# Value stage: 768 gathered and 1280 dense columns, and the coefficients' low halves made by GpSimd

## The reference, cut to what matters

```python
def peer_ffn(x, wq, subkeys, u, v):          # x: 256 tokens x 2048
    ...                                      # 8 heads x 16 experts = 128 slots per token, out of 16384
    act = gelu(einsum('td,tkd->tk', xc, u[ec]))
    return einsum('tk,tkd->td', gc * act, v[ec])
```

## Time and profile before

| | us |
|---|---|
| median of 3 runs | 1769.39 (1768.2 to 1777.46) |
| profiled execution, its own time | 1779.1 |
| its span (first to last instruction) | 1777.3 |
| value stage in it, first issue to last product | 1188.4 to 1671 |
| busy over the span: PE, DVE, ACT, GpSimd | 1265.5, 1466.0, 808.6, 873.6 |

### The profile page before, as it was taken

One profiled execution on the slowest core, in us unless ns is written; L12 is line 12 of the kernel. 1 busy time (PEld: TensorE's weight loads), 2 busy tenths in 40 slices (PEclk: granted clock), 3 DMA queues, 4 the chain that ended last, 5 costly groups with the idle time before them and its releaser, 6 DMA issues.

```text
span 1777.3 us, 22600 instructions
## 1 busy us (share of the span) xinstructions
PE 1265.5 (71%) x7003; PEld 1129.7 (64%) x7003; DVE 1466.0 (82%) x1984; ACT 808.6 (45%) x1403; POOL 873.6 (49%) x872
## 2 busy tenths in 40 slices
PE   9999999999992460000122222399999999999997
PEld 9899998989982430000111122289999999999887
DVE  6636666754578998999999999889999999999856
ACT  6324446644210121111777777684444444444654
POOL 1100000000154546666766677488888888888303
PEclk9999999999996685555555555599999999999999
DMA  9954444367899999999999999819999999999953
GB/s 303 332 196 147 143 143 143 121 235 263 317 372 422 417 404 423 413 409 422 421 421 416 414 414 422 360 50 383 378 381 376 383 376 378 379 373 382 349 192 117
DMA packets 120101, 577.12 MB, mean 325 GB/s; under 512 B 14596, under 2 KB 29269, under 8 KB 78688
## 3 DMA queue, kind: packets, MB, share of 16 engines
q0 software_dynamic: 58544, 367.16, 51.1%
q1 hardware_dynamic: 61488, 209.10, 32.9%
HBM read 571.99 MB, written 7.36 MB: 326 GB/s over the span
## 4 chain that ended last, share of the span: by engine, by line
PE 59%; DVE 12%; DMA 11%; issue 10%; POOL 5%; ACT 1%; SPq 1%; DVEq 0%; POOLq 0%; ACTq 0%
PE banks L2339 17%; PE banks L2346 9%; PE banks L1929 7%; DVE rows L1695 6%; DMA rows<-peer_u_dram,expert 6%; PE banks L1985 6%; PE banks L2008 5%; PE banks L2230 4%; DMA early_rows<-peer_u_dram,expert 3%; PE banks L1987 3%; PE banks L2312 2%; POOL rows L797 2%; PE banks L1949 1%; DVE early_rows L1695 1%; POOL pick L739 1%
## 5 line engine op out<-in xcount | busy, mean ns | idle before, releaser
L1695 DVE SCALAR_TENSOR_TENSOR rows<-rows,banks 128x2048 f32<-128x2048 f32 x206 | 466.2, 2281 | 39.2 <-DMA rows<-peer_u_dram,expert 38.5
L849 POOL DMA_INDIRECT vrow<-peer_v_gathered_dram,vidx x224 | 342.6, 1529 | 73.1 <-issue 44.9
L797 POOL DMA_INDIRECT rows<-peer_u_dram,expert x206 | 197.7, 960 | 340.1 <-DVE expert L1732 154.2
L2312 PE MATMUL banks<-hots 128*128 128x128 f32 x512 | 103.0, 370 | 233.8 <-ACT hots L1239 229.5
L2312 PEld LDWEIGHTS banks<-hots 128*128 128x128 f32 x512 | 90.2, 266 | 246.8 <-issue 177.8
L1797 DVE SCALAR_TENSOR_TENSOR hres<-vrow,slot_coef,hres 128x704 f32<-128x704 f32 x224 | 211.9, 946 | 4.5 <-DMA vrow<-peer_v_gathered_dram,vidx 4.2
L1811 DVE TENSOR_TENSOR vlo<-vraw,vhi 128x1344 fp32r<-128x1344 f32 x128 | 198.8, 1553 | 2.2 <-ACT vhi L1287 1.7
L913 ACT CAST whi<-raw 128x2048 fp32r<-128x2048 f32 x77 | 146.8, 1906 | 116.0 <-PE banks L1929 67.3
L2339 PE MATMUL banks<-vhi,chi 128*128 128x448 f32 x762 | 179.2, 370 | 2.9 <-ACT vhi L1287 2.9
L2339 PE MATMUL banks<-vhi,clo 128*128 128x448 f32 x762 | 179.0, 370 | 0.0
L2346 PE MATMUL banks<-vlo,chi 128*128 128x448 f32 x762 | 178.6, 369 | 0.0
(11 more groups left out here) (301 smaller groups left out, 2761.7 us busy)
## 6 DMA issues: line engine op xcount, KB each, us to landing
vraw<-peer_v_dense_dram SPq DMA_DIRECT2D x128, 672.0 KB
raw<-w_in_packed_dram SPq DMA_DIRECT2D x42, 1024.0 KB, 4.8
raw<-w_out_dram SPq DMA_DIRECT2D x16, 1024.0 KB, 5.4
raw<-ple_gate_dram SPq DMA_DIRECT2D x16, 1024.0 KB, 5.5
wqraw<-peer_wq_packed_dram SPq DMA_DIRECT2D x12, 1024.0 KB, 9.6
wq_ahead<-peer_wq_packed_dram SPq DMA_DIRECT2D x4, 1024.0 KB, 6.3
vrow<-peer_v_gathered_dram,vidx POOLq DMA_INDIRECT x224
rows<-peer_u_dram,expert POOLq DMA_INDIRECT x208, 16.7
```

The source lines that it names most:

```text
L797: pool.indirect_dma_start(dst[:, :], None, peer_u[0], bass.IndirectOffsetOnAxis(ap=expert[b][:, k:k + 1], axis=0))\
L849: pool.indirect_dma_start(vrow[j][:, :], None, v_gathered, bass.IndirectOffsetOnAxis(ap=idx[:, j % TT, j // TT:j // TT + 1], axis=0))\
L1695: dve.scalar_tensor_tensor(out=r[:, :], in0=r[:, :], scalar=1.0, in1=xps[tt][:, :], op0=ALU.mult, op1=ALU.mult, accum_out=dots[b][:, k:k + ...
L2312: last = pe.matmul(bank[SPREAD_BANK[m]][:, a * P:(a + 1) * P], hot2[tt][m][:, a, :], hot1[tt][m][:, a, :], start=True, stop=True)
```

## The change

Three things. The gathered columns become 768 and the dense ones 1280, in blocks of 448, 448 and 384. From chunk 8 on the halves of the coefficients are made for two chunks at a time, in new tiles `chi_pair` and `clo_pair` that lie over the part of `spread` already used: ACT makes the high halves (`chi_of_pair`), and GpSimd, no longer DVE, makes the low ones (`clo_of_pair`), a subtraction on 128 x 512 elements, between two row issues: for chunks c and c+1 (c even) behind the issues of slot c+2 and ahead of those of slot c+3. It waits for the high halves and for PE's high products of chunk c-3. The first 8 chunks keep the old functions. ACT's `vhi` waits in addition for DVE's `vlo` of chunk c-2. Some small tiles move, so that the longer last row buffer covers nothing that is still needed.

```diff
-VGATH = 704
+VGATH = 768
-VCOLS = [448, 448, 448]
+VCOLS = [448, 448, 384]
...
+    chi_pair = [at(f"chi_pair{b}", (32 + 2 * b) * KB, [P, TT, 2, P], f32r) for b in range(2)]
+    clo_pair = [at(f"clo_pair{b}", (96 + 2 * b) * KB, [P, TT, 2, P], f32r) for b in range(2)]
...
+            def clo_of_pair(c, b):
+                pool.wait_ge(chi_ready, c + 2)
+                pool.wait_ge(v_hi_mm, c - 2)
+                pool.nop(nofuse=True)
+                pool.tensor_tensor(clo_pair[b][:, :, :, :], spread[:, :, bass.ds(c, 2), :],
+                                   chi_pair[b][:, :, :, :].bitcast(fp32), ALU.subtract).then_inc(clo_ready, 2)
...
                     if not first and j % TT == 0:
                         pool.wait_ge(v_used, TT * c0 + j + TT - VROWS)
                         pool.nop(nofuse=True)
+                        if j // TT % 2 and lows[j // TT // 2]:
+                            clo_of_pair(c0 + j // TT - 3, 1 - j // TT // 2)
                     pool.indirect_dma_start(vrow[j][:, :], None, v_gathered, ...
...
+            def chi_of_pair(i, r):
+                c = VBODY * i + r
+                act.wait_ge(v_lo_mm, c - 2)
+                act.copy(chi_pair[r // 2 % 2][:, :, :, :], spread[:, :, bass.ds(c, 2), :]).then_inc(chi_ready, 2)
+            def high_rows(i, r):
+                c = VBODY * i + r
+                act.wait_ge(v_landed[r % VRING], 16 * (VBODY // VRING * i + r // VRING + 1))
+                act.wait_ge(v_hi_mm, c - 1)
+                act.wait_ge(vlo_ready, c - 1)
+                act.copy(vhi[r % 2][:, :], vraw[r % VRING][:, :]).then_inc(vhi_ready, 1)
...
             with act.Fori(1, V_TURNS) as i:
-                for r in range(VBODY):
-                    v_halves(i, r)
+                for r in range(0, VBODY, 2):
+                    chi_of_pair(i, r)
+                    high_rows(i, r)
+                    high_rows(i, r + 1)
...
+            def low_rows(i, r):
+                c = VBODY * i + r
+                use_v_row(i, r, 0, False)
+                dve.wait_ge(vhi_ready, c + 1)
+                dve.tensor_tensor(vlo[r % VRING][:, :], vraw[r % VRING][:, :], vhi[r % 2][:, :].bitcast(fp32),
+                                  ALU.subtract).then_inc(vlo_ready, 1)
+                use_v_row(i, r, 1, False)
...
             with dve.Fori(1, V_TURNS) as i:
                 for r in range(VBODY):
-                    v_lows(i, r)
+                    low_rows(i, r)
```

More of the change, by code:

```diff
@@ L313, in build @@
     bidxf = place("bidxf", [P, 2, TOPK])
+    picked = place("picked", [P, 2, TOPK])
+    expert = [place(f"expert{b}", [P, TOPK], i32) for b in range(2)]
+    gexp = [place(f"gexp{b}", [P, TOPK]) for b in range(2)]
     slot_row = place("slot_row", [P, TT * SLOTS], i32)
@@ L875, in _ @@
             pool.wait_ge(side_dotted, PEER_STEPS - SIDE_FROM + 1)
-            v_fetch(0, 0, first=True)
-            v_fetch(0, 1)
-            with pool.Fori(1, V_TURNS - 1) as i:
+            v_fetch(0, 0, first=True, lows=(False, False))
+            v_fetch(0, 1, lows=(False, False))
+            v_fetch(1, 0, lows=(False, True))
+            v_fetch(1, 1)
+            with pool.Fori(2, V_TURNS - 1) as i:
                 v_fetch(i, 0)
@@ L882, in _ @@
             v_fetch(V_TURNS - 1, 1, last=True)
+            clo_of_pair(NKEYS - 2, 1)
             pool.wait_ge(clo_ready, NKEYS)
@@ L2327, in v_block, with halves_of @@
                 return bank[tt * VBLK + VBLK - 1 - b][:, 0:VCOLS[b]], v_blocks[b]
+            def halves_of(i, r):
+                if isinstance(i, int) and i == 0:
+                    return chi[r % 2][:, :, :], clo[r % 2][:, :, :]
+                return chi_pair[r // 2 % 2][:, :, r % 2, :], clo_pair[r // 2 % 2][:, :, r % 2, :]
             def v_products(i, r, first=False):
                 c = VBODY * i + r
+                hi, lo = halves_of(i, r)
                 pe.wait_ge(vhi_ready, c + 1)
-                for x in (chi[r % 2], clo[r % 2]):
-                    if x is clo[r % 2]:
+                for x in (hi, lo):
+                    if x is lo:
                         pe.wait_ge(clo_ready, c + 1)
@@ L2338, in v_products @@
                             dst, cols = v_block(tt, b)
-                            last = pe.matmul(dst, x[:, tt, :], vhi[r % 2][:, cols], start=first and x is chi[0],
+                            last = pe.matmul(dst, x[:, tt, :], vhi[r % 2][:, cols], start=first and x is hi,
                                              stop=False, skip_group_check=True)
@@ L2345, in v_products @@
                         dst, cols = v_block(tt, b)
-                        last = pe.matmul(dst, chi[r % 2][:, tt, :], vlo[r % VRING][:, cols], start=False, stop=False,
+                        last = pe.matmul(dst, hi[:, tt, :], vlo[r % VRING][:, cols], start=False, stop=False,
                                          skip_group_check=True)
@@ L2361, in _ @@
             r = VBODY - 1
+            hi, lo = halves_of(V_TURNS - 1, r)
             for b in range(VBLK):
@@ L2364, in _ @@
                     dst, cols = v_block(tt, b)
-                    for n, (x, v) in enumerate(((chi, vhi[r % 2]), (clo, vhi[r % 2]), (chi, vlo[r % VRING]))):
-                        last = pe.matmul(dst, x[r % 2][:, tt, :], v[:, cols], start=False, stop=n == 2,
+                    for n, (x, v) in enumerate(((hi, vhi[r % 2]), (lo, vhi[r % 2]), (hi, vlo[r % VRING]))):
+                        last = pe.matmul(dst, x[:, tt, :], v[:, cols], start=False, stop=n == 2,
                                          skip_group_check=True)
```

12 lines of the change are left out of this document (5 added, 7 removed).

## The result

The changed kernel takes 1842.6 us (median of 4 runs, 1834.15 to 1855.21) against 1769.2 us before: a ratio of 1.041, interval 1.038 to 1.044. It is slower by 73 us. Its profiled execution took 1844.79 us, 65.7 more than that of before. From here on that execution is meant by "after".

The account below looks back on a forecast made before the run. PE set the pace; after the change GpSimd would, at 4.1 us a chunk: +49.5 for 120 chunks, -4.5 for its lead, -1 for the first 8 chunks, net +44, 1813.4 us, said as 1814; range 1764 to 1858.

Parts of the forecast that it names:

- the two layouts: Value stage: cycles laid out with row landing delays of 7.0 and 4 us, 3.93 and 4.48 us a chunk, 1793 to 1860.
- If PE alone decided: Value stage: PE's chunk falls from 3.72 to 3.55 us; 128 chunks would give back 22 us.
- DVE's held time: Value stage: GpSimd's subtraction holds DVE off for 1.05 us in two chunks, 0.53 a chunk.
- partly hidden: Rival, value stage: the exclusion costs DVE less than 1.05 us; 3.63 to 3.78 us a chunk, 1758 to 1777; chance 0.08.
- The floor of 7.61 us a pair: Value stage: DVE's work of 3.28 us plus 0.53 held by GpSimd, at least 3.81 us a chunk.
- GpSimd's cycle: Value stage: four issues at 1.26 us plus about 1.3 for the subtraction, 6.3 us for two chunks undisturbed, plus waits for DVE.
- The landing delay: Value stage: rows land 7.0 us after their access with loaded DMA engines, 3.6 otherwise; moves the period by half a microsecond.
- The mis-sized term: Value stage: GpSimd's period of 4.1 us a chunk, 492 us for 120 chunks instead of 442.5, so +49.5.
- GpSimd's lead over the last use: End of the value stage: GpSimd's finish ahead of the last row's use shrinks from 10.2 to about 5.7 us, -4.5.
- PE as the bound: Rival, value stage: GpSimd uses DVE's idle moments and PE stays the bound, faster; -22 us, 1748; chance 0.18.
- Only the subtraction excludes DVE: Rival, value stage: issues aren't held; DVE is the bound at 3.81 us a chunk, +11, 1780; chance 0.15 shared with DMA.
- The DMA engines: Rival, value stage: DMA is the bound at 379 GB/s, 3.80 us a chunk, 1779; chance 0.15 shared with DVE.

Follow-up runs that it names:

- e1: The kernel before with only the new column split (768 gathered; blocks 448, 448, 384), coefficient halves made the old way: ratio 1.0067 to the kernel before, 1785.3 us.
- e3: The changed kernel with the low halves of two chunks made by DVE in one 128x512 subtraction, not by GpSimd: ratio 1.0216 to the kernel before, 1811.9 us.
- e7: The changed kernel with DVE's `vlo` made in two instructions of 640 columns: ratio 1.0464 to the kernel before, 1852.8 us.
- e8: e3 with DVE's `vlo` made in two instructions of 640 columns: ratio 1.0239 to the kernel before.
- e9: The kernel before with eight memsets of 8 columns added on GpSimd between the issues, every second slot: ratio 1.0009 to the kernel before.
- e4: The changed kernel with eight GpSimd memsets, which read nothing, in place of its subtraction: ratio 1.0145 to the kernel before, 1800.8 us.
- e5: The changed kernel with GpSimd's subtraction halved to 128x256, one token tile, PE's work unchanged: ratio 1.0334 to the kernel before, 1834.5 us.
- e11: e3 with DVE's subtraction cut in two, 128x256 ahead of each chunk's first row: ratio 1.0079 to the kernel before, 1786.4 us.

## Why the prediction was right, point by point

The sign, the main mechanism (GpSimd's subtraction holds DVE, and GpSimd, without idle time, holds the others) and the order of size were right: 1842.6 lies in the range of 1764 to 1858, and 44 us were forecast where 73 came (in the profiled executions 65.7). That the mean period came between the two layouts of 3.93 and 4.48 a chunk is in part luck. Both were steady cycles; from one even chunk's `vlo` to the next, after has pairs from 7.60 to 10.73 us, less and more than either.

**PE.** 64 columns less in a third of the matmuls were to make its chunk 3.55 us. In the undisturbed stretches of after, its sixes start 1.16 and 1.17 us apart (1430.04, 1431.20, 1432.37), about 3.5 a chunk: right, and worth nothing. The step that failed here is the reading of what the gain would be with the halves left alone: "If PE alone decided" it would be 22 us, and e1 shows that it didn't decide alone. DVE's own chunk went from 3.55 to 3.60 us, above PE's, which alone leaves at most 0.12 of the saving, and pauses ahead of late rows took that too (3.71).

**DVE's held time.** Forecast 1.05 us a pair, from two lines at the kernel's end. Measured: (1213 - 1012) ns x 224 rows and (1575 - 1480) ns x 120 `vlo` are 56.4 us, 0.94 for each of 60 pairs, and 1.05 with the rows of the last buffer counted in. That a multiply-add is held like a tensor_tensor, the doubt behind the rival "partly hidden", is settled by the row of 2.13 us. The floor of 7.61 us a pair (2 x 3.28 + 1.05) is also there: from one even chunk's `vlo` to the next, 18 of 59 pairs take 7.60 to 7.67, none less, and the others up to 10.73.

**The subtraction.** Taken as 1.28 us from the earlier trace rows, median 1.289. But the sign that the subtractions would average "well over 1.28 us" didn't come: 54 of the 60 took 1.27 to 1.33 us and six 1.68 to 1.71, a mean of 1.33. GpSimd was seldom held there; the waiting sits in its issues.

**GpSimd's cycle.** Forecast 6.3 us undisturbed and 1.9 of waits and holds, 8.2 a pair. Measured over 1240 to 1640 us: issues 5.82, subtraction 1.34, `vidx` 0.31, gaps 1.01, together 8.5, with no gap above 0.31 us; waiting inside the four issues is 2.0. That is the forecast picture, GpSimd without idle time and the others waiting. The landing delay was taken as 7.0 us from the earlier trace rows, from an issue's access (its end less 0.82) to the use. Counted in the same way it is 6.9 in after (median of the 51 rows that DVE waited over 0.1 us for; the 6.9 of the view of `vrow` is from the issue's start).

**The mis-sized term** is the period: 4.1 us a chunk was forecast, 4.23 came. From GpSimd's first issue of chunk 8 to the end of its last it took 507.4 us for 120 chunks, where the sum had 492. Timeline of GpSimd after, and the last use of a row:

```profile
1216.85 0.95 POOL L862 DMA_INDIRECT vrow<-peer_v_gathered_dram,vidx  x1 [0.30 <-DVE hres L1829]
...
1723.18 1.09 POOL L862 DMA_INDIRECT vrow_last<-peer_v_gathered_dram,vidx  x1 [0.30 <-issue]
...
1732.24 1.01 DVE L1829 SCALAR_TENSOR_TENSOR hres<-vrow_last,slot_coef,hres 128x768 f32<-128x768 f32 x1
```

The other terms are read from the same rows. GpSimd's lead over the last use is 8.0 us (1732.24 less 1724.27), where it was to shrink from 10.2 to 5.7: 2.3 us. (The 5.7 has no row behind it; the forecast's own delay of 7.0 less 0.82 gives 6.2.) The first 8 chunks were to give back 1 us and lost 2.4 (1216.85 against 1214.42 in the earlier trace rows): 3.4. With the period's 15.4 that is 44 + 21.1 = 65.1 us, beside the 65.4 by which the span grew. The remaining 7.5 us of the miss lie in the subtraction of 9.7 us for the median: before's profiled execution was that much above its median, after's only 2.2.

**What the argument had wrong though its number held.** Two things. It let GpSimd in at the next boundary of DVE, and e3, e7 and e8 show boundaries that are passed over. And it called GpSimd the bound, full in itself. e9, made from the kernel before, shows that its waits give way, and e4 against e5 that time in which GpSimd reads costs more than time in which it is merely busy. A better account, which these runs support but don't prove: the two engines hold each other in turn, GpSimd inside its issues and DVE during the subtraction, and the period is what one round of this takes.

**The rivals.** PE as the bound (1748) and "partly hidden" fall with the lengthened rows. "Only the subtraction excludes DVE" (1780) falls with issues of 1.50 us and a mean of 1440 ns; the inference of the Trainium skill (SBUF — State Buffer, Who interferes with whom) that descriptor generation isn't held by a tensor_tensor led there, and the issue of 2.96 us in e3, which ends 0.82 after a `vlo`, speaks against it as the earlier trace rows did. The DMA engines moved 388 GB/s in e1, so at 337 they weren't the bound. For e1, at a share of 1.00, no run excludes them.

## What to carry to other kernels

Before work is moved to an engine that "has time", look at what its long instructions wait for: here GpSimd's issues were waiting for moments of DVE, and the subtraction took 1.3 us of GpSimd and about 1 us of DVE, where each of the two chunks' `clo` had cost DVE 0.34. Moving it saved DVE 0.7 us a pair and cost it 1.0. And making one instruction of two on an engine that another one must slip past can cost more than it saves (e3 against e11, 1.4%): look at where the other gets in, not only at the busy time.

## What the hardware showed that was not expected

- **A boundary between two DVE instructions isn't always an opening for GpSimd.** Ahead of a multiply-add a waiting issue always got in; ahead of a tensor_tensor it was passed over up to 57 times in 72 (e8, between the halves of `vlo`). The cause is open.
- **PE can come back slower from a pause.** PE waited 3.60 us for `clo_pair` and then took 2.41 and 1.94 us for six matmuls that otherwise take 1.33 (timeline of after, then windows of it; PEclk stands third from the right):

```profile
1424.89 2.41 PE L2387 MATMUL banks<-vhi,clo_pair 128*128 128x448 f32 x6 [3.60 <-POOL clo_pair L845]
...
1430.04 1.33 PE L2387 MATMUL banks<-vhi,clo_pair 128*128 128x448 f32 x6
```

```profile
1421.00:1424.80 3.80, 0.29 (x2) 0.00 (x0) 3.44 (x3) 0.00 (x0) 3.78 (x2) 1.00 1.01 361
1424.80:1427.00 2.20, 2.11 (x6) 1.94 (x7) 1.43 (x2) 0.00 (x0) 1.74 (x3) 0.55 0.49 193
...
1429.00:1432.00 3.00, 3.00 (x18) 2.81 (x17) 3.00 (x3) 0.56 (x1) 2.68 (x3) 1.00 0.74 203
```

  The granted clock was 0.55 in the 2.2 us after the pause, near the lower of its two levels (1.2 of 2.4 GHz), and 1.00 again from 1429. Over the stage it is 0.97. It isn't so after every pause: of the 25 pauses of PE over 1 us between 1220 and 1735 us, seven were followed by slow matmuls, and 18 weren't, among them four of 2.62 to 3.28 us. The prediction had no term for this; what it cost wasn't measured by itself.
- **Small memsets on GpSimd are short in a row**: eight of 8 columns took 0.37 us (e9), eight of 64 columns 0.77 (e4), and DVE's rows beside the latter stayed at 1015 ns.
